# First projection by input tiles over all tokens, with earlier small transfers and matmuls on a cleared tile

## What is computed

```
h = rms_norm(x, ln_pre_mix)            # x: 512 tokens x 1024
proj = h @ w_in                        # columns for four mixers and their gates
dcq, dckv, dkr                         # 416 of these columns: the latents of mixer D
bias = t5_table[bucket]                # relative position bias, used in mixer B only
... four attentions A, B, C, D; each branch -> 1024, gated by sigmoid(gate_logits), summed, @ w_out
x = x + rms_norm(mixer)
x = x + rms_norm(swiglu(rms_norm(x)))
```

## Time and profile before

| | us |
|---|---|
| median of three runs | 1697.42 (1696.83 to 1698.2) |
| profiled execution, own time | 1697.18 |
| its span, first to last instruction | 1695.4 |
| PE busy in the span | 1665.8 (98%) |
| POOL busy | 1095.0 (65%) |
| DVE busy | 830.2 (49%) |
| ACT busy | 465.8 (27%) |

### The profile page before, as it was taken

One profiled execution on the slowest core, in us unless ns is written; L12 is line 12 of the kernel. 1 busy time (PEld: TensorE's weight loads), 2 busy tenths in 40 slices (PEclk: granted clock), 3 DMA queues, 4 the chain that ended last, 5 costly groups with the idle time before them and its releaser, 6 DMA issues. The chain is left out here.

```text
span 1695.4 us, 22074 instructions
## 1 busy us (share of the span) xinstructions
PE 1665.8 (98%) x8582; PEld 1397.8 (82%) x8582; DVE 830.2 (49%) x1488; ACT 465.8 (27%) x1063; POOL 1095.0 (65%) x1211
## 2 busy tenths in 40 slices
PE   7999999999999999999999999999999999999997
PEld 6888788877898888888987887988779988888886
DVE  6654558665556444410266545686564564443002
ACT  3451422434251111100155415134342411111000
POOL 8636457553669777677685365564546797776774
PEclk9999999999999999999999999999999999999999
DMA  5213222221222222222242131222112222222222
GB/s 217 75 50 112 82 81 75 75 75 50 100 76 100 100 100 100 84 87 102 95 139 75 50 120 55 100 75 75 55 70 79 97 99 100 100 99 77 101 87 84
DMA packets 27335, 151.40 MB, mean 89 GB/s; under 512 B 3483, under 2 KB 6811, under 8 KB 13376
## 3 DMA queue, kind: packets, MB, share of 16 engines
q1 hardware_dynamic: 22928, 140.70, 23.2%
q10 hardware_dynamic: 4304, 9.30, 1.8%
HBM read 147.88 MB, written 4.70 MB: 90 GB/s over the span
## 5 line engine op out<-in xcount | busy, mean ns | idle before, releaser
L561 POOL TENSOR_SCALAR w_hi<-raw 128x512 fp32r<-128x512 f32 (+3 forms) x576 | 367.1, 647 | 576.0 <-DMA raw<-stream 576.0
L565 POOL TENSOR_TENSOR w_lo<-raw,w_hi 128x512 fp32r<-128x512 f32 (+3 forms) x576 | 710.4, 1244 | 0.0
L613 PE MATMUL work<-h_hi,w_hi 128*128 128x512 f32 (+1 forms) x576 | 218.5, 379 | 1.3 <-DVE h_lo L1445 1.0
L614 PE MATMUL work<-h_lo,w_hi 128*128 128x512 f32 (+1 forms) x576 | 217.3, 377 | 0.0
L615 PE MATMUL work<-h_hi,w_lo 128*128 128x512 f32 (+1 forms) x576 | 217.3, 377 | 0.0
L738 PE MATMUL main<-h_hi,w_hi 128*128 128x512 f32 x512 | 208.3, 407 | 0.0
L738 PE MATMUL main<-h_lo,w_hi 128*128 128x512 f32 x512 | 207.1, 404 | 0.0
L738 PE MATMUL main<-h_hi,w_lo 128*128 128x512 f32 x512 | 205.4, 401 | 0.0
L613 PE MATMUL work<-act_hi,w_hi 128*128 128x512 f32 (+1 forms) x396 | 145.0, 366 | 0.0
L614 PE MATMUL work<-act_lo,w_hi 128*128 128x512 f32 (+1 forms) x396 | 144.7, 365 | 0.0
L615 PE MATMUL work<-act_hi,w_lo 128*128 128x512 f32 (+1 forms) x396 | 144.7, 365 | 0.0
(11 more groups left out here) (334 smaller groups left out, 3242.9 us busy)
## 6 DMA issues: line engine op xcount, KB each, us to landing
raw<-stream SPq DMA_DIRECT2D x106, 1024.0 KB, 4.8
raw<-stream SPq DMA_DIRECT2D x32, 704.0 KB, 4.0
raw<-stream SPq DMA_DIRECT2D x4, 832.0 KB, 4.5
x<-x_in ACTq DMA_DIRECT2D x4, 512.0 KB, 11.7
t_line<-t_first ACTq DMA_DIRECT2D x2, 1024.0 KB
rpb<-rpb_line ACTq DMA_DIRECT2D x32, 64.0 KB, 3.0
bias_b<-t_line ACTq DMA_DIRECT2D x2, 768.0 KB, 4.4
out<-x SPq DMA_DIRECT2D x6, 256.0 KB, 2.2
```

The lines of the kernel that those rows point to most:

```text
L561: pool.tensor_scalar(w_hi[:, slot, parts[q]], raw[:, slot, parts[q]], 1.0, 0.0, ALU.mult, ALU.add).then_inc(piece_hi, 1)
L565: e = pool.tensor_tensor(w_lo[:, slot, part], raw[:, slot, part], w_hi[:, slot, part].bitcast(F32), ALU.subtract)
L613: pe.matmul(dst, a_hi, b_hi, start=first, stop=False, **kw)
L614: pe.matmul(dst, a_hi, b_lo, start=False, stop=False, **kw)
```

## The change

1. **Latents of the first layer by input tile.** For each `k`, PE runs all four token tiles (12 matmuls) instead of two passes over halves. ACT makes `h_hi` and the squares 512 wide, DVE makes `h_lo` 512 wide and sums all squares itself, one tile behind; POOL sums none in the first layer's first norm. The second layer keeps its halves.
2. **Quarter signals.** POOL signals each quarter of the first three pieces of a layer (`quarter_split`), and PE waits by quarter. The first piece comes in four transfers, and there POOL's subtraction follows its copy directly.
3. **Small transfers.** The norm gains of both layers lie in one block of their own, `gains_in`, the first transfer of ACT. x comes in eight transfers. SP asks for the second piece only when x tile 1 has landed.
4. **Cleared tile.** DVE clears `warm` (128 x 512). PE runs 14 matmuls on it into `main[1]` at the start, ACT one activation between the issues of x tiles 3 and 4.
5. **t5 moved.** `hot` and `t5` are issued behind x; the t5 matmul stands behind the first four gate steps and writes `main[1]`; DVE's copy stands behind its sums; ACT waits for that copy before it squares the latents. `t5_line` and `bias_b` are made in the first layer only, `bias_b` behind the gates of mixer D.

```diff
+WARM = 14
@@ SP
+                    if l == 0 and n == 0:
+                        for q in range(QUARTERS):
+                            part = slice(N_LAT * q, N_LAT * q + N_LAT)
+                            sp.dma_start(raw[:, 0, part], stream[0, :, part]).then_inc(first_in[q] if q < QUARTERS - 1 else piece_in[0], 16)
+                        sp.wait_ge(x_loaded[1], 16)
+                        continue
                     sp.dma_start(raw[:, slot, 0:size], stream[l * NP_ + n, :, 0:size]).then_inc(piece_in[slot], 16)
-                    if l == 0 and n == 0:
-                        sp.dma_start(gain_in[:, :, :], params_in[:, :, 0:KD].rearrange("l p c -> p l c")).then_inc(gains_in_place, 16)
@@ POOL, split
+                lag = 0 if first else 1
+                for q in range(QUARTERS + lag):
                     if q < QUARTERS:
+                        if first:
+                            pool.wait_ge(first_in[q] if q < QUARTERS - 1 else piece_in[0], 16)
                         pool.tensor_scalar(w_hi[:, slot, parts[q]], raw[:, slot, parts[q]], 1.0, 0.0, ALU.mult, ALU.add).then_inc(piece_hi, 1)
...
+                        if n < SLOTS and q - lag < QUARTERS - 1:
+                            e.then_inc(quarter_split, 1)
@@ POOL, input_sum
-                if (l, name, half) == (0, "pre_mix", 1):
+                if (l, name) == (0, "pre_mix"):
                     pool.sem_inc(in_sum, KD - 1)
@@ PE
-            pe.wait_ge(t5_loaded, 32)
-            pe.matmul(work[0][0:4, :], t5[:, :], hot[:, :], start=True, stop=True).then_inc(t5_mm, 1)
-            pe.wait_ge(t5_copied, 1)
+            pe.wait_ge(warm_ready, 1)
+            for _ in range(WARM):
+                pe.matmul(main[1][:, :], warm[:, 0:P], warm[:, :], start=True, stop=True)
...
+                if l == 0:
+                    for k in range(KD):
+                        wait_quarter(0, k // 4, k % 4)
+                        pe.wait_ge(lo_done, 2 * k + 2)
+                        for t in range(NT):
+                            latent_part(k, t)
...
                 gate_steps(l, "D", 0)
+                if l == 0:
+                    pe.wait_ge(t5_loaded, 32)
+                    pe.matmul(main[1][0:4, :], t5[:, :], hot[:, :], start=True, stop=True).then_inc(t5_mm, 1)
                 pe.wait_ge(loaded, 16)
                 input_square(l, "pre_mix")
@@ ACT
+                for d in range(KD):
+                    act.wait_ge(x_loaded[d], 16)
...
+                    act.activation(h_hi[:, d, :], x[:, d, :], ACT.Copy, scale=gain_in[:, 0, d:d + 1]).then_inc(hi_done, 2)
+                    act.activation(norm_f["sq"][:, d, :], x[:, d, :], ACT.Square).then_inc(in_squared, 2)
...
+            act.dma_start(gain_in[:, :, :], gains_in).then_inc(gains_in_place, 16)
+            for d in range(KD):
+                act.dma_start(x[:, d, :], x_in[:, d, :]).then_inc(x_loaded[d], 16)
+                if d == 3:
+                    act.wait_ge(warm_ready, 1)
+                    act.activation(r_tmp[:, 0:1], warm[:, 0:1].bitcast(F32), ACT.Copy)
             act.dma_start(hot[:, :], hot_in).then_inc(t5_loaded, 16)
             act.dma_start(t5[:, :], t5_in).then_inc(t5_loaded, 16)
...
-                act.wait_ge(t5_sem, 16 * l + 16)
-                act.dma_start(t5_line, ...
+                if l == 0:
+                    act.wait_ge(t5_copied, 1)
+                    act.dma_start(t5_first, t5_row[:, :]).then_inc(t5_sem, 16)
 
                 act.wait_ge(pv_done, at(l, 9, 1))
                 act.wait_ge(work_done, at(l, N_WORK, 3))
@@ DVE
+            dve.memset(warm[:, :].bitcast(F32), 0.0).then_inc(warm_ready, 2)
...
+                for d in range(KD):
+                    dve.wait_ge(hi_done, 2 * d + 2)
...
+                    dve.scalar_tensor_tensor(out=h_lo[:, d, :], in0=x[:, d, :], scalar=gain_in[:, 0, d:d + 1], in1=h_hi[:, d, :].bitcast(F32),
+                                             op0=ALU.mult, op1=ALU.subtract).then_inc(lo_done, 2)
+                    if d:
+                        add(d - 1)
+                add(KD - 1)
+                dve.wait_ge(t5_mm, 1)
+                dve.tensor_copy(t5_row[:, :], main[1][0:4, :]).then_inc(t5_copied, 1)
```

More of the change, by code:

```diff
@@ L314, in program @@
     act_lo = sb("act_lo", [P, KF, S], F32R, Z + 44 * K)
-    hot = sb("hot", [33, BIAS_X], F32, QT)
-    t5 = sb("t5", [33, 4], F32, QT + 2 * K)
-    t5_row = sb("t5_row", [4, BIAS_X], F32, QT + 4 * K)
+    warm = sb("warm", [P, S], F32R, Z + 20 * K)
+    hot = sb("hot", [33, BIAS_X], F32, KT + 12 * K)
+    t5 = sb("t5", [33, 4], F32, Z + 96 * K)
+    t5_row = sb("t5_row", [4, BIAS_X], F32, KT + 14 * K)
     V = Z + 88 * K
@@ L385, in program @@
         loaded = sem("loaded")
-        x_loaded = [sem(f"x_loaded{i}") for i in range(KD // 2)]
+        x_loaded = [sem(f"x_loaded{d}") for d in range(KD)]
+        first_in = [sem(f"first_in{q}") for q in range(QUARTERS - 1)]
+        quarter_split = sem("quarter_split")
+        warm_ready = sem("warm_ready")
         piece_in = [sem(f"piece_in{i}") for i in range(SLOTS)]
@@ L628, in wait_main @@
                 if m < 2:
+                    if (l, m) == (0, 1):
+                        pe.wait_ge(t5_copied, 1)
                     return
@@ L732, in gate_steps @@
                         wait_main(l, m)
-                        if j % 2 == 0:
+                        if j % 2 == 0 and (of, j) != ("D", 0):
                             wait_piece(l, PIECE[f"gate{of}{j // 2}"])
+                    if (of, j, which, k % 2) == ("D", 0, 0, 0):
+                        wait_quarter(l, PIECE["gateD0"], k // 2)
                     slot = PIECE[f"gate{of}{j // 2}"] % SLOTS
@@ L884, in _, with latent_part @@
             for l in range(0, L):
-                for half in range(2):
-                    if l and half:
+                def latent_part(k, t):
+                    a, slot = N_LAT * (k % 4), k // 4
+                    mm = three(lat_bank[t][:, 0:N_LAT],
+                               h_hi[:, k, P * t:P * t + P], h_lo[:, k, P * t:P * t + P],
+                               w_hi[:, slot, a:a + N_LAT], w_lo[:, slot, a:a + N_LAT], k == 0, k == KD - 1)
+                    if k == KD - 1:
+                        mm.then_inc(pv_done if t == 1 else work_done, 1)
+                    elif (k, t) == (3, 3):
+                        mm.then_inc(lat_half, 1)
+                if l == 0:
[4 more added lines that the diff above has]
+                            latent_part(k, t)
+                for half in range(2) if l else ():
+                    if half:
                         spread(l - 1, "post_ffn", 1)
@@ L890, in _ @@
                     for k in range(KD):
-                        if half == 0 and k % 4 == 0:
-                            wait_piece(l, PIECE[f"Dlat{k // 4}"])
+                        if half == 0:
+                            wait_quarter(l, k // 4, k % 4)
                         wait_split(l, ("h", "pre_mix", half, k))
-                        a, slot = N_LAT * (k % 4), k // 4
                         for t in (2 * half, 2 * half + 1):
[L896 to L903, removed]
+                            latent_part(k, t)
+                        if (half, k) == (0, 1):
                             mean_square(l - 1, "post_ffn", 1)
                 gate_steps(l, "D", 0)
+                if l == 0:
+                    pe.wait_ge(t5_loaded, 32)
+                    pe.matmul(main[1][0:4, :], t5[:, :], hot[:, :], start=True, stop=True).then_inc(t5_mm, 1)
                 pe.wait_ge(loaded, 16)
@@ L1170, in first_input @@
             def first_input():
[L1172 to L1176, removed]
+                for d in range(KD):
+                    act.wait_ge(x_loaded[d], 16)
+                    for half in range(2):
+                        assert next(splits) == ("h", "pre_mix", d // 4, 2 * d % KD + half)
+                    act.activation(h_hi[:, d, :], x[:, d, :], ACT.Copy, scale=gain_in[:, 0, d:d + 1]).then_inc(hi_done, 2)
+                    act.activation(norm_f["sq"][:, d, :], x[:, d, :], ACT.Square).then_inc(in_squared, 2)
             def next_input(l, name, half, d, done, banks):
@@ L1528, in first_input, with add @@
             def first_input():
[L1530 to L1538, removed]
+                sq, total = norm_f["sq"], norm_f["sum"][:, :]
+                def add(d):
+                    if d:
+                        dve.wait_ge(in_squared, 2 * d + 2)
+                        if d > 1:
+                            dve.wait_ge(first_sum, d - 1)
+                        dve.tensor_tensor(total, sq[:, 0, :] if d == 1 else total, sq[:, d, :], ALU.add).then_inc(first_sum, 1)
+                for d in range(KD):
+                    dve.wait_ge(hi_done, 2 * d + 2)
+                    for half in range(2):
+                        assert next(splits) == ("h", "pre_mix", d // 4, 2 * d % KD + half)
```

(10 more changed lines are left out.)

38 lines of the change are left out of this document (21 added, 17 removed).

## The result

The changed kernel takes 1705.41 us (median of 5 runs, 1704.95 to 1706.6), the kernel before, run beside it, 1697.0 (5 runs, 1696.55 to 1698.2): a ratio of 1.0049 with an interval of 1.0034 to 1.0064. It is 8.4 us slower. The prediction was 1695.3 in a range from 1691.8 to 1698.6, so it is wrong in sign and size. The profiled execution after took 1706.6 (span 1704.8), 9.4 more than that of before.

The account below looks back on a forecast made before the run. PE, busy 98% of the span, was taken to bound the kernel. 1697.18 us, less 4.2 for an earlier start of the gate matmuls, plus 2.3 for a new wait behind it, gave 1695.3, range 1691.8 to 1698.6.

Parts of the forecast that it names:

- [39.16]: Start, in us, of the first gate matmul behind the norm-factor spread before; gains or losses by then were to reach the end whole.
- each DVE instruction waits for one POOL instruction: Port contention at the input split: h_lo takes 1.51 us beside POOL's subtraction, 0.48 alone, and adds 0.17 to POOL's instruction.
- First `h_hi` at 7.3: Kernel start: ACT's first h_hi begins at 7.3 us after 13 queued transfer issues, bounds 5.3 and 8.6.
- First matmul at 9.2: Kernel start: PE's first projection matmul at 9.2 us instead of 12.13, from 7.2 to 10.5.
- the clock was low as forecast: First projection matmuls: after about 3.5 us of PE idle the clock is low again, costing 1.3 us as before.
- Second piece at 12.4: First layer: second weight piece lands at 12.4 us, quarters ready from 14.8 to 22.0, ending the 1.3 us wait at 19.14.
- rival 3: First-layer input tiles: port contention spaces h_lo by 2.7 us, over 17 us for seven; 1699.1 us, chance 0.12.
- L at 28.55: Start of the first layer's gate matmuls, 32.78 us before, forecast at 28.55, 4.2 us earlier.
- The new wait: Before the spread: ACT's squares wait for the t5 copy, PE idles about 2.1 us; price 2.3 us, bounds 0.2 and 3.8.
- Its lower bound of 0.2: Least price of holding the squares: only the t5 matmul less the old wait, if the factor chain were hidden.
- The second layer's quarter signals at nothing: Second layer: PE starts tile 4 earlier, but tile 7 needs its h_lo; only 0.1 of the 1.16 us wait is gained.

Follow-up runs that it names:

- experiment 1: Changed kernel with the r_token copy replaced by an instruction with one PSUM input and one SBUF input: 1697.71 us, 0.9996 of the kernel before.
- 3: Changed kernel, copy untouched, with POOL made to wait in layer 0 for the r_token copy before splitting the fourth piece: 1697.3 us, 0.9993 of before.
- 13: Changed kernel, copy untouched, with POOL's subtractions in layer 0's gateD1 directly following their own copies, leaving small gaps: 1697.64 us, 0.9994 of before.
- experiment 4: Changed kernel, copy untouched, with ACT squaring the latents before it waits for the t5 copy: 1705.11 us, 1.0026 of before.
- experiment 10: Experiment 1 plus a four-wide SBUF maximum on DVE among the input's h_lo and sums, behind tile 6's h_lo: 1696.38 us, 0.9992 of before.
- experiment 5: Changed kernel with both the PSUM-input r_token and ACT's squares ahead of the t5 wait: 1695.92 us, 0.9987 of before.
- 14: Kernel before, plus a 256-wide DVE maximum of two SBUF tiles behind the r_token copy in the first layer: 1697.64 us, 0.9999 of before.
- experiment 8: Experiment 6 with 22 matmuls on the cleared tile instead of 14: 1692.63 us, 0.9965 of before.
- experiment 7: Experiment 6 with no matmuls on the cleared tile instead of 14: 1694.65 us, 0.9976 of before.
- experiment 6: Experiment 5 with ACT issuing hot, t5, const and rpb_line behind its first-input activations instead of ahead: 1693.81 us, 0.9975 of before.

## Why the prediction was wrong

The step that failed is a sentence: "Behind [39.16] PE has no long wait until the second layer, so what is won or lost by 39.16 reaches the end whole." It was read off the trace of before and taken to hold after. But the change moved both parties behind that mark. POOL, without six microseconds of sums, reached each later piece some 2 us earlier (its split of `gateD1` starts at 37.23, before at 39.19), and DVE's factor chain, held by ACT's new wait, ended at 38.11 as it had at 38.28. So the copy left the end of one piece's split and fell into the middle of the next. Experiments 1, 3 and 13 show that this meeting is the loss; that the shift alone made the copy lose is argued, since in experiment 4 it is passed over from the old place too. I had priced the two engines against each other for `h_lo` and sums only, and counted the 0.17 us copy as the end of a chain, without a range.

Against the mechanism itself: I wrote that "each DVE instruction waits for one POOL instruction". That holds nearly everywhere in these traces (18.59 in experiment 10, 465.10 after) and fails once in each slow kernel, in the first layer. The Trainium skill, "SBUF — State Buffer", section on the two separate sides, says that whichever starts first, a GpSimd operation or a DVE operation of the kinds it lists (with two SBUF inputs, for one), holds the shared ports for its whole instruction, and that the other is blocked. The traces show that the wait need not end with that instruction: the copy is passed over for six further POOL instructions in a row (38.40 to the two at 42.06).

The other steps, in their order:
- First `h_hi` at 7.3: 8.05. Thirteen issues stood ahead of it, as said, but they took longer together: the last ended at 7.93. First matmul at 9.2: 10.34. Its starts were 0.35 apart up to 13.25 (eleven in 3.5 us in the window), so the clock was low as forecast.
- Second piece at 12.4: it landed at 15.27, 2.9 late. No tile waited for it all the same; the alternation of DVE and POOL kept ahead of PE, and rival 3 did not happen.
- L at 28.55: 29.89. Won 2.9, forecast 4.2; 1.1 of the difference is the late start.
- The new wait: the first gate matmul behind the spread at L + 8.7, found 8.64; PE's idle 2.1, found 1.69. ACT's squares began behind DVE's `t_row` copy, as said. Right in place and size (the mark moved by 8.64 - 6.38 = 2.26); experiments 1 and 5 price it at 1.5 to 1.8 us, forecast 2.3. Its lower bound of 0.2 does not follow from its own terms: 0.9 for the t5 matmul less the old wait of 0.55 is 0.35.
- The second layer's quarter signals at nothing: there PE waits 0.78 for `h_lo` where it waited 1.16 for `w_lo`, and the 2.62 that followed is still there, at 2.6. Right.
- By these steps the changed kernel should be 0.6 us ahead at 39, and, with the copy mended, experiment 1 is so (0.0004 of 1697 us, 0.7, within its interval of none). Every term of the sum came out within 1.5 us, and what was no term cost 7.7 (the medians of after and experiment 1) to 9.0 (their ratios); the rows give 5.9 + 2.2.

The range held only the terms that I had named. Rival 3 had the right resource, the port, at the wrong place, before L; its condition (seven `h_lo` over 17 us) left out everything behind L.

What stays open: what lets such an instruction in, and why it was shut out here alone. A visible gap does (13), POOL standing does (3), a PSUM input avoids the question (1). But the copy of before, the instruction of 14, the copy of the second layer (885.25) and the sum at 465.10 got in without one. Experiments 4 and 14 are the sharpest pair: in both the instruction stands from the middle of the same piece's last two subtractions on (36.88, and 38.2), and in 14 it enters at that piece's end, in 4 it is passed over there and to the end of the next piece, and three of the twelve runs of 4 have times without the loss. Whether this is a race finer than these rows or lies in what POOL's next instruction waits for, no run tells.

The best version, experiment 8, is 1692.63 us, 0.9965 (0.9953 to 0.9978) of before: the change, with the copy through PSUM, the squares ahead of the wait, the four issues behind the input, and 22 matmuls on the cleared tile.

## What to carry to other kernels

When a change moves POOL's or DVE's work in time, list the SBUF instructions of DVE on the critical path behind it, however short, and look what POOL does at their new time. Most wait for one POOL instruction; one here waited to the end of POOL's unbroken run, over 6 us, and the traces do not say how to tell it beforehand. Give such an instruction an operand in PSUM, or leave POOL a gap; both cost nothing here. And a sentence such as "nothing behind this point changes" is a term of the sum and wants a bound like any other.

## What the runs showed of the hardware

- At one place, in a gapless run of POOL instructions on SBUF, a DVE instruction with SBUF operands only lasted 6.24 to 8.14 us instead of 0.17, to the end of that run; four columns and 256 alike, copy and two-input form alike. Elsewhere such instructions waited for one POOL instruction (1.63 at 465.10, 1.04 at 18.59 in experiment 10), and none lasted over 2.3.
- With a POOL gap of 0.09 us it took 0.28; one operand in PSUM made it 0.16.
- Matmuls on a cleared tile: 22 that reach the first real one gave 1.2 us between the medians against fourteen followed by 2 us of idle PE (ratio intervals overlapping), and 2.0 us against none. Fourteen against none: 1693.81 and 1694.65, intervals overlapping. The granted clock of such windows read 1.00 (experiment 7), 0.50 (6) or 0.56 (after) with ten or eleven starts in 3.4 to 3.5 us in each; early in the kernel the count of starts is the surer reading.
- What an idle of PE of 2 to 3.3 us behind those fourteen did to the clock varied. Low from the first matmul on: after 2.01 us (experiment 6) and 3.07 (after). High for the first few starts, then low: after 2.48 (experiment 5, first matmul at 10.16, starts 0.35 apart from 11.12 on). High throughout: after 3.28 (experiment 1's profiled execution, 1695.34, the lowest of its runs; first matmul at 9.66, starts 0.19 apart). The length of the idle alone does not decide.
